# The first query unit's matmuls spread over an earlier RWKV phase, in a fused three-layer kernel on one Trainium2 core

## The reference, cut to what matters

```python
h = rms_norm(x, norm_mix_pre)
z = h @ w_in                        # RWKV columns, attention columns (queries first), gate columns
o_a = rwkv7_time_mix(z_rwkv, ...)   # per head: state = state*w + (state a) b + v k;  y = state r
o_b = nsa_attention(z_nsa, ...)     # queries: (z_q * 64**-0.5), 16 heads of 64
m = g_a * (o_a @ w_branch_rwkv) + g_b * (o_b @ w_branch_nsa)
x = x + rms_norm(m @ w_out, norm_mix_post)
... then a convolved gated feed-forward, and two more layers (attention, feed-forward)
```

## The kernel before

| | unit 16 | unit 17 | unit 18 |
|---|---|---|---|
| ACT | phase 6, behind level 2 of the powers | start of phase 7 | phase 7, between `take_u` 2 and `split_one(20)` |
| DVE | phase 6, behind `take_r` 2 | start of phase 7, behind `take_r` 0 | phase 7, behind `take_state` 2 |

## Time and profile before

### The profile page before, as it was taken

One profiled execution on the slowest core, in us unless ns is written; L12 is line 12 of the kernel. 1 busy time (PEld: TensorE's weight loads), 2 busy tenths in 40 slices (PEclk: granted clock), 3 DMA queues, 4 the chain that ended last, 5 costly groups with the idle time before them and its releaser, 6 DMA issues.

```text
span 1423.4 us, 27091 instructions
## 1 busy us (share of the span) xinstructions
PE 1346.5 (95%) x10342; PEld 1173.9 (82%) x10342; DVE 899.2 (63%) x1750; ACT 641.7 (45%) x1240; POOL 281.6 (20%) x341
## 2 busy tenths in 40 slices
PE   7999999899899989999998989899999999899998
PEld 6898888789778888999987955588888886788886
DVE  5666666645658876778846444667654765577654
ACT  4344444433134434676635334544343576443433
POOL 0002322212334340223301021111210122022200
PEclk9999999999799989999998968999999999899999
DMA  7312111024312125455555420255555451255452
GB/s 298 120 63 87 62 61 61 32 64 148 146 63 75 72 75 185 156 177 180 191 189 183 165 85 31 89 178 185 198 181 203 148 178 60 90 184 200 179 204 90
DMA packets 26774, 189.90 MB, mean 133 GB/s; under 512 B 2960, under 2 KB 3088, under 8 KB 4400
## 3 DMA queue, kind: packets, MB, share of 16 engines
q1 hardware_dynamic: 25632, 182.51, 35.9%
q0 software_dynamic: 1040, 5.96, 1.4%
HBM read 186.37 MB, written 1.05 MB: 132 GB/s over the span
## 4 chain that ended last, share of the span: by engine, by line
PE 86%; DVE 7%; ACT 3%; DVEq 1%; issue 1%; DMA 1%; POOL 0%; POOLq 0%; ACTq 0%; SPq 0%
PE ps L569 33%; PE ps L517 13%; PE ps L597 11%; PE ps L599 6%; PE ps L832 5%; PE ps L679 1%; PE ps L668 1%; PE ps L851 1%; PE ps L1073 1%; PE ps L549 1%; PE ps L542 1%; PE ps L486 1%; PE ps L541 1%; PE ps L797 1%; PE ps L931 1%
## 5 line engine op out<-in xcount | busy, mean ns | idle before, releaser
L1369 ACT ACTIVATE w_hi<-ring 128x1024 fp32r<-128x1024 f32 x125 | 132.6, 1061 | 319.0 <-PE ps L569 177.8
L597 PE MATMUL ps<-h_both,w_hi 128*128 128x512 f32 x704 | 246.8, 394 | 2.0 <-DVE h_both L1867 2.0
L1897 DVE TENSOR_TENSOR w_lo<-ring,w_hi 128x1024 fp32r<-128x1024 f32 x117 | 145.4, 1243 | 136.1 <-ACT w_hi L1369 135.9
L599 PE MATMUL ps<-h_both,w_lo 128*128 128x256 f32 x704 | 198.1, 281 | 0.0
L569 PE MATMUL ps<-h_both,w_hi 128*128 128x256 f32 x1008 | 185.6, 287 | 2.3 <-DVE h_both L1867 2.3
L569 PEld LDWEIGHTS ps<-h_both,w_hi 128*128 128x128 f32 x1008 | 160.4, 196 | 3.3 <-issue 3.3
L597 PEld LDWEIGHTS ps<-h_both,w_hi 128*128 128x128 f32 x704 | 132.8, 189 | 32.1 <-issue 2.6
L1903 DVE TENSOR_TENSOR w_lo<-ring,w_hi 128x1024 fp32r<-128x1024 f32 x117 | 147.4, 1260 | 0.0
L517 PE MATMUL ps<-oT_r,ring_r 128*128 128x256 f32 x512 | 146.3, 286 | 0.0
L569 PE MATMUL ps<-h_both,w_lo 128*128 128x256 f32 x504 | 144.3, 286 | 0.0
L599 PEld LDWEIGHTS ps<-h_both,w_lo 128*128 128x128 f32 x704 | 134.2, 191 | 0.0
(11 more groups left out here) (411 smaller groups left out, 2946.2 us busy)
## 6 DMA issues: line engine op xcount, KB each, us to landing
ring<-in_weights SPq DMA_DIRECT2D x170, 1024.0 KB, 4.8
arena<-in_aux POOLq DMA_DIRECT2D x1, 2112.0 KB, 12.8
grow<-in_rows POOLq DMA_DIRECT2D x3, 512.0 KB, 4.4
cst<-in_consts SPq DMA_DIRECT2D x1, 1497.5 KB, 15.1
x<-in_x SPq DMA_DIRECT2D x1, 1024.0 KB, 4.9
arena<-in_swbias POOLq DMA_DIRECT2D x1, 1024.0 KB, 7.1
arena<-arena POOLq DMA_DIRECT2D x1, 1024.0 KB, 9.0
out<-xn SPq DMA_DIRECT2D x4, 256.0 KB, 2.3
```

Source lines behind the costliest of these rows:

```text
L597: pe.matmul(bank[:].rearrange("p (a t) -> p a t", a=2), hi, h_both[:, :, k, :], start=k == 0, stop=False)
L599: m = pe.matmul(bank[:, 0:S], lo, h_hi[:, k, :], start=False, stop=k == KT - 1)
L1369: act.activation(w_hi[:, half_of(u0, m), WH:], ring[:, (u0 + m) % RING, WH:], ACT.Copy).then_inc(w_hi_p, 1)
L1897: dve.tensor_tensor(w_lo[:, half_of(u0, m), WH:], ring[:, (u0 + m) % RING, WH:], w_hi[:, half_of(u0, m), WH:].bitcast(F32), ALU.subtract). ...
```

## The change

Phase 5 gets eight pieces (unit 16): one in each of slots 1, 2, 5 and 9, four in slot 11, just ahead of `grams(7)`. Phase 6 gets eight (unit 17) instead of 14, phase 7 ten instead of 14. Slot 0 has none in the three phases. Six pieces are left for the tail: two, `center(7)`, two, `variance(7)`, two. ACT copies unit 16 out at the start of phase 6, right behind `rows(7)`, instead of after level 2 of the powers; DVE does so right behind its `take_r` 0, instead of behind `take_r` 2. The number of pieces, all operations and all operands stay the same.

```diff
@@ rwkv_phase(n) of PE @@
-                fill = rwkv_dense(n + 3) if n + 3 < PAIRS else q_fill if n >= PAIRS - 2 else iter(())
+                fill = rwkv_dense(n + 3) if n + 3 < PAIRS else q_fill
+                pieces = {PAIRS - 3: {1: 1, 2: 1, 5: 1, 9: 1, 11: 4},
+                          PAIRS - 2: {1: 1, 3: 1, 5: 2, 7: 1, 9: 1, 10: 1, 11: 1},
+                          PAIRS - 1: {1: 1, 2: 1, 3: 1, 4: 1, 5: 1, 6: 1, 7: 1, 8: 1, 10: 1, 11: 1}}.get(n)
...
-                    if slot == 0:
+                    if slot == 0 and pieces is None:
                         next(fill, None)
...
-                    next(fill, None)
-                    if slot == 5:
+                    for _ in range((2 if slot == 5 else 1) if pieces is None else pieces.get(slot, 0)):
                         next(fill, None)
                 if front:
                     grams(n + 2)
-                if n < PAIRS - 2:
+                if pieces is None:
                     for _ in fill:
                         pass
@@ behind the phases @@
-            next(q_fill, None)
+            for _ in range(2):
+                next(q_fill, None)
             center(PAIRS - 1)
@@ rwkv_phase(n) of ACT @@
                 if powers:
                     rows(n + 1)
+                if n == PAIRS - 2:
+                    take_query(0)
                 if front:
                     take_vg(n + 2)
...
-                if n == PAIRS - 2:
-                    take_query(0)
                 if powers:
                     take_powers(n + 1, 3)
@@ rwkv_phase(n) of DVE @@
                 if scan:
                     take_r(n, 0)
-                if n == PAIRS - 1:
-                    take_query(1)
+                if n >= PAIRS - 2:
+                    take_query(n - PAIRS + 2)
                 dve.drain()
...
                     take_r(n, 2)
-                if n == PAIRS - 2:
-                    take_query(0)
```

## The result

The changed kernel takes 1418.83 us (median of 12 runs, 1413.81 to 1426.57) where the kernel before took 1426.49 in the same timing (12 runs, 1421.74 to 1430.68). The ratio is 0.9944, with a 95% interval from 0.9923 to 0.9966: faster by 8.0 us, 4.9 to 11.0. The forecast was 1422.0, with a range from 1419.8 to 1424.8. The profiled execution took 1419.35 us with a span of 1417.5.

A forecast was written before the change was run, and what follows sets the result against it. The prediction took PE, busy for 95% of the span, as the bound. Phase 5 +1.5, phase 6 -5.5, phase 7 and tail +0.1 gave -3.9, stated as -4.0: 1426.0 - 4.0 = 1422.0 us, range 1419.8 to 1424.8.

The forecast's parts named there:

- the small waits: Phase 5: PE's 0.55 us wait ahead of `scan_r` 1 and smaller ones before slot 9, forecast to vanish under added pieces.
- the 2.22 us: Phase 5: PE's wait for DVE ahead of `grams(7)`, forecast to vanish because PE would arrive last.
- the 1.34: End of phase 5: PE's 1.34 us wait for ACT's two copies ahead of phase 6's `scan_r`, forecast to stay.
- slots 2, 5 and 9 at 0.91: Phase 5: price of 0.91 us for each lone piece in these slots, within 6.44 us for eight pieces.
- Clock: 1.55 forecast: `grams(7)` in phase 5: without the wait ahead, PE's clock stays full and the fall's 1.55 us is saved.
- the rival by which the 1.55 us would be missing in before: Clock gives nothing: fall absent in before's median, or due in a new phase 7 wait; 1423.6 us, chance 0.18.
- Neither chain: Phase 6: copies between levels of the powers, and links of the scan; neither forecast to surface as waits, cost zero.
- The four new waits: Phase 7: PE waits of 1.07 (`scan_u` 0), 1.22 (`scan_u` 2), 0.65 (after slot 8) and 0.68 us (`scan_state` 3).
- as a block: From unit 20 on, everything follows by semaphores and only shifts, with no load later.
- the pieces surface on the scan: Phases 6 and 7: lost cover makes scan steps wait 0.5 us per chunk, 4 us in all; 1426.0, chance 0.13.
- Slower: Phase 7: a long low-clock stretch costs 6.4 us, with no gain in phase 5 either; 1430.0 us, chance 0.08.
- More: Phase 7: some of the four waits overlap work counted on PE; up to -5.7 us, 1420.3, chance 0.06.

The follow-up runs named there:

- clock-only: The kernel before with 18 overwritten-result matmuls added in PE's wait ahead of `grams(7)`, nothing moved; ratio to before 0.9971, and 0.9977 in a second timing.
- five edited forms of the changed kernel: Changed kernel with two pieces behind `grams(7)` (0.9951), eight in slot 11 (0.9969), two phase 7 splits halved (0.9946), first and third together (0.9930), 42 matmuls added (0.9998).
- padded: The changed kernel with 42 matmuls (5.0 us), whose results are overwritten, added ahead of unit 20; ratio to before 0.9998.

## Why the prediction came out as it did

**Phase 5: +1.5 forecast, +0.9 measured.** The covers held: the small waits and the 2.22 us are filled, the 1.34 stay, and DVE wasn't the bound ahead of `grams(7)`. Too high was the term "slots 2, 5 and 9 at 0.91". The 0.91 us of the earlier trace rows is a piece between 64-row matmuls of the powers. In slot 9 the piece lies between L797, itself 128x128, and the powers: 269.58 - 268.34 = 1.24 us, of which L797 takes 0.54 (269.53 to 270.07 before), so 0.70. In slot 5 it is 0.75 in the same way, in slot 1 0.64; slot 2 has 0.90, slot 11 3.07. Together 6.06 us for 6.44. Another 0.2 us lies in groups that stood ahead of a wait in before. There the busy time counts their last matmul to its end; now the next matmul starts before that end. A level of 48 costs 1.55 us instead of 1.61, `variance` 0.54 instead of 0.61, `scan_state` 3 0.26 instead of 0.34. One reading of the prediction was off without a price: DVE's list slipped by 1.0 us and not by 0.3 (its last addition ends 21.14 us into the phase, for 20.16), and PE still came last.

**Clock: 1.55 forecast, 1.50 measured** by the clock-only kernel. The fall hung on the wait, and the rival by which the 1.55 us would be missing in before is not borne out: both of its profiled executions have it. Its other half came once: in one of three profiled executions of the changed kernel the clock fell behind the wait of 1.01 us, and cost 28.76 - 27.30 = 1.46 us. The other two, and the five edited forms of the changed kernel, kept it with the same wait at the same place. That agrees with the rule that the prediction quotes from the Trainium skill, TensorE: Matmul & The Clock Gate, "Part 1: The HAM clock gate": the same kernel meets the transition at different points.

**Phase 6: -5.5 forecast, -5.7 measured.** Neither chain surfaced; idle time is 0.15 us as before, and the moved copies cost nothing. The two pieces of slot 0 were under-priced this time: with none between, level 0 and `scan_u` run on as one group.

```profile
278.65 1.26 PE L832 MATMUL ps<-arena 64*64 64x64 f32 x36
279.84 0.70 PE L780 MATMUL ps<-pT,cst 128*128 128x256 f32 x2
```

That is 1.19 us for what took 1.34 in two parts.

**Phase 7 and tail: +0.1 forecast, -0.15 measured** at full clock. The four new waits come to 3.35 us for 3.62. The largest error is on `scan_state` 3 (0.51 for 0.68).

So the sum that should have stood there is +0.9 - 5.7 - 0.15 = -5.0 us. The step that failed up to unit 20 is a size: one price for every lone piece, and some 0.3 us too much of waits. It makes 1.1 of the missing microseconds. Had it been the only error, the median would be 1426.5 - 5.0 = 1421.5, inside the range.

**From unit 20 on "as a block".** This is the other step that didn't hold, and it has more weight: the prediction put everything behind unit 20 at nothing. Three timings of the changed kernel say 8.0, 5.6 and 6.6 us, 6.7 in the mean, for 5.0 up to unit 20. The intervals of the second and the third (4.4 to 8.8 us) hold 5.0, and that of the first just does (4.9 to 11.0), so the first timing's 8.0 us shouldn't be read as the size of the effect. But in all nine timings of edited kernels other than the padded one the ratio lies below what the stretch gives, by 0.6 us (three of them) up to 3 us.

In the traces the rest isn't of one length: 1091.0 and 1093.3 us in two executions of before, 1090.7 to 1091.5 in three of the changed kernel, 1086.9 and 1088.9 in two of clock only. Its first stretch, from `spread_variance(7)` to the next norm's transposes (L486), for before twice and clock only twice:

```profile
332.53:571.57 239.04, 220.13 (x1488) 195.65 (x1487) 166.77 (x452) 90.61 (x212) 74.23 (x60) 0.94 0.31 110
332.01:571.10 239.09, 220.19 (x1488) 195.65 (x1487) 166.90 (x452) 90.61 (x212) 74.21 (x60) 0.94 0.31 109
330.93:567.30 236.37, 217.43 (x1489) 193.43 (x1488) 166.90 (x452) 90.61 (x212) 74.22 (x61) 0.96 0.32 111
330.52:567.90 237.38, 218.76 (x1489) 195.12 (x1487) 166.74 (x452) 90.51 (x212) 74.22 (x61) 0.96 0.31 110
```

The matmuls are the same but for one, DVE and ACT are as busy as before, and most of the difference in length is PE's busy time, at a higher mean clock. Over all twelve profiled executions this stretch takes 236.3 to 237.4 us where some 17 us of it are at the lower clock, 238.8 to 239.4 where some 27 are, and 237.3 to 238.4 in between. Clock only moves nothing behind `grams(7)`, so this is the clock and not an order of work. The timings point the same way: the mean granted clock of clock only's executions is 0.9695 and 0.9688, of before's beside them 0.9654 and 0.9645; the one fall that the kernel is rid of, 3.4 us long, accounts for 0.0012 of that. The changed kernel had 0.9669 and 0.9671 in its second and third timing, against the same 0.9654 and 0.9645.

So the prediction's error here is that it let the clock's falls behind unit 20 stay as they were, and in the traces they don't: their number and length vary from execution to execution. Why they are fewer in the edited kernels, the padded one (0.9686 for 0.9664) included, stays open; no run isolates it. That the padded kernel's ratio is 0.9998 all the same speaks against a gain behind unit 20 that the change itself makes.

**The rivals.** That the pieces surface on the scan is out: phase 6 has no wait over 0.15 us, and the new waits of phase 7 come to less than was counted. Slower is out: the one fall seen in phase 7 cost 1.46 us, where that rival needed a low stretch that costs more than the whole gain. *More* named 1420.3, which is nearer to the median than the forecast is, but not by its mechanism: the waits overlapped only 0.3 us more than was counted, of the 1.7 that it needed.

## What to carry to other kernels

In a schedule written out by hand, price a filler by its neighbours: here a piece of six full matmuls cost 0.91 us between quarter-array matmuls and 0.70 beside full ones. Fillers are worth most in a wait behind which the clock falls, where the wait and the fall are both won, and next where an engine's list holds a long operation ahead of a link of the chain; cutting that operation in two (1.7 us here) did more than the placing of pieces. Before a difference of a few us is read as the size of an edit, compare the stretch that it touches, which here repeated to 0.02 us, while the executions of one kernel within a timing lay 4 to 13 us apart. And before a remainder is put down to the edit, compare the granted clock of the stretches that it doesn't touch.

## What the runs showed that was not expected

A feed-forward loop has two paces at the same clock. The stretch from 955 to 989 us lies in the second layer's feed-forward units; in the view of stretches it reads for the kernel before

```profile
955.00:989.00 34.00, 34.00 (x198) 29.98 (x198) 23.90 (x31) 14.38 (x19) 6.92 (x13) 1.00 0.52 186
```

and for the changed kernel

```profile
955.00:989.00 34.00, 34.00 (x194) 29.44 (x194) 23.36 (x30) 13.88 (x18) 6.81 (x12) 1.00 0.53 186
```

PE is busy throughout in both, with 198 and with 194 matmuls of the same code: 2% apart. At the faster pace the whole stage, from its first norm transposes (L486 of before) to the next stage's, takes 187.3 us, at the slower one 189.6. The same kernel shows both: the changed one had 189.6, 189.6 and 187.3 in its three profiled executions. The padded kernel's 191.6 us are the slower pace and a fall of the clock, with a granted clock of 0.53 from 918 to 925.

The slower pace costs the kernel next to nothing, though, since the stage behind it took 120.1 us in place of 122.1. In the view of stretches that stage reads for before

```profile
1105.40:1227.50 122.10, 111.97 (x677) 92.11 (x678) 74.42 (x187) 72.21 (x171) 24.22 (x17) 0.94 0.38 125
```

and for the changed kernel

```profile
1102.40:1222.50 120.10, 106.96 (x676) 88.01 (x677) 74.38 (x187) 72.11 (x171) 24.16 (x17) 1.00 0.38 127
```

In the four executions at the slower pace other than the padded one the clock didn't fall there, and both stages together take 309.7 us for 309.4. What sets the pace, and why the falls behind it are missing, wasn't found. The scatter of the whole kernel comes more from two other places: the stretch ahead of the first norm's transposes (236.3 to 239.4 us) and the last feed-forward stage, from its norm to the end (193.6 to 198.3 us).
